# Second mixing stage: an earlier third weight load, weights split behind the product two rows ahead, and the decay chain and the heads five rows later

## The chip, the cores and the metric

The kernel runs on one NeuronCore of a Trainium2 chip. The metric is device time in microseconds (us) of one execution of the whole program; lower is better. TensorE (PE) multiplies, VectorE (DVE) and ScalarE (ACT) prepare operands and take results away, GpSimd (POOL) and SyncE (SP) start most transfers. The engines run their own instruction streams in order and wait for each other by semaphores.

## What is computed

The reference is two transformer blocks on 512 tokens of width 1024 in float32. The change touches only one stage of the second block, the first projections of its mixing and the gated delta rule behind them:

```python
h = modulate(x, g_mix[l], sh2, sc2)
proj = h @ w_in[l]
q_lat, kv_lat, k_pe, gq, gk, gv, ga, gb, gz, gates = jnp.split(proj, split_at, axis=-1)
...
qkv = jax.nn.silu(causal_depthwise_conv(qkv, w_conv))
q = l2norm(to_chunks(q, DK)) * (DK ** -0.5)
k = l2norm(to_chunks(k, DK))
beta = jax.nn.sigmoid(b.astype(f32))
g = -jnp.exp(a_log.astype(f32)) * jax.nn.softplus(a.astype(f32) + dt_bias.astype(f32))
decay = jnp.cumsum(g, axis=-1)
...
A = jnp.where(strict, jnp.einsum('bhnid,bhnjd->bhnij', k_beta, k) * L, 0.0)
T = lax.linalg.triangular_solve(A + eye, ...)
w = jnp.einsum('bhnij,bhnjd->bhnid', T, k_beta * jnp.exp(decay)[..., None])
u = jnp.einsum('bhnij,bhnje->bhnie', T, v * beta[..., None])
```

## The kernel before

**Rows.** The projection is done in 57 *rows*, numbered 0 to 56: each takes 128 columns of `w_in` against all of `h` and leaves one 128x512 result in PSUM bank 0 or 1 in turn. float32 is kept by splitting each operand into a rounded part and a rest: for row n, ScalarE rounds the weights (`w_hi`, line 222, tile `Wh`), VectorE makes the rest (`w_lo`, line 234, tile `Wl`), and TensorE runs 24 matmuls (`pe_three`, lines 242 to 244). There are two split slots, so `w_hi` of row n+2 can start only when the product of row n is done, and four raw slots, filled by SP's `w_load`. Row 0 and the small tile `t_ab` (40 columns: the heads' a and b) are multiplied together in `pe_two` (lines 427 to 430) while `h` is still being made piece by piece, eight pieces k.

Rows 0 to 5, 11 to 16, 25 to 30 and 39 to 44 are the key, query and value of two heads each. For these VectorE runs a four-tap convolution (`conv_dve`, lines 2523 and 2526), ScalarE a SiLU and, for key and query, a square (lines 2493, 2499); TensorE sums the squares over the partitions (line 2463), ScalarE takes the root (2484), VectorE the reciprocal and a diagonal (2547, 2549), TensorE spreads it (2451), and VectorE scales (2540). The other rows are latents, output gates and branch gates, which ScalarE takes away (lines 2777, 2506, 2514).

**Decay chain.** From the `t_ab` product come beta (sigmoid on ScalarE, line 2375) and the decays: abs, exp, ln, exp on ScalarE (2378 to 2383), then five operations on VectorE (2400 to 2408, mark `lx`), then 12 small transposes on TensorE (`decay_pe`), and the copies of `decay_act` and `decay_dve`. The heads need all of it.

**Heads.** Each of eight heads is a generator in 14 parts on TensorE, ScalarE and VectorE. In the *opening* TensorE spreads the decays of the head (lines 2602, 2603) and turns the values (171); VectorE subtracts and masks (2712 to 2717); ScalarE exponentiates and scales (2660 to 2669). The *second part* is the key-by-key and key-by-query products (2612, 2614, 171). In the *third part* VectorE makes the start of the triangular inverse (2724 to 2732) and TensorE turns it (line 2288, first 16 matmuls). Ten parts of doubling steps (2632, 2288, 2641) and a last part (2647, 2650) follow.

**Order.** `row_steps` writes the order out: step n holds the front of row n (its product on TensorE, norms), then one part of each of at most two live heads, then the back of row n (convolution or taking away). At most one head is started in a step, when the row of its values is past; head h+2 starts when head h has ended. The heads start in steps 3, 6, 17, 20, 31, 34, 45 and 48. Behind the rows six products for the keys of the other branch (line 251) are interleaved with the last head parts.

**Queues.** SP issues `t_ab` and rows 0 and 1, waits for the end of the stage ahead, then for all of `h`, and then issues a 512 KB constant (`sel8`), the 2 MB save of X (`x_out`), row 2 and the rest. `delta_act` starts with a wait for `x_out` on ScalarE, ahead of the rows' own loop; in the kernel before, row 2's split stands ahead of it in `mix2_act`.

Of the kernel before, what the change touches and what calls it, by code (L numbers as in the profile page):

```python
# [96 lines left out]
def build(nc, a, out, upto="end"):  # L97
# [285 lines left out]
    class Modulated:  # L383
# [33 lines left out]

        def pe_two(self, e, outs, ts, ms, keys):

            w = [[x.rearrange("p (k m) -> p k m", k=8) for x in w_parts(i)] for i in ts]  # L420
            steps = [(t, k) for k in range(6) for t in (0, 1)] + [(t, k) for t in (0, 1) for k in (6, 7)]
            for i in ts:
                V.wait_ge(e, ("w", i))
            for t, k in steps:
                o, (hi, lo) = outs[t][0:ms[t], :], w[t]
                A.wait_ge(e, (self.tag, "hi", k))
                e.matmul(o, hi[:, k, :], self.hi[:, k, :], start=k == 0, stop=False)
                e.matmul(o, lo[:, k, :], self.hi[:, k, :], start=False, stop=False)
                V.wait_ge(e, (self.tag, "lo", k))
                ins = e.matmul(o, hi[:, k, :], self.lo[:, k, :], start=False, stop=k == 7)  # L430
                if k == 7:
                    PE.then_inc(ins, ("w", ts[t]), keys[t])
# [1778 lines left out]
    NCX = 2  # L2211
# [108 lines left out]
    def mix2_sp(e):  # L2320
        for i in [t_ab] + t_row[0:2]:
            w_load(e, i)
        behind(e, "ffn1")
        con2_in.then_inc(e.dma_start(con1[:, 768:1344], a["consts"][:, 2048:2624]), "con2")
        A.wait_ge(e, ("m2", "hi", 7))
        V.wait_ge(e, ("m2", "lo", 7))
        sel_in.then_inc(e.dma_start(sel8, a["consts"][:, 3072:4096]), "sel")
        x_out.then_inc(e.dma_start(XD, X_t), "x")
        for i in t_row[2:] + t_uk:
            w_load(e, i)  # L2330

    def mix2_pe(e):
        m2n.root_pe(e)
        n4.pe_two(e, [ps(2), ps(0)], [t_ab, t_row[0]], (40, 128), ["ab", ("row", 0)])

# [34 lines left out]
    def mix2_act(e):  # L2370
        R = CX[0][0]
        n4.act(e)
        w_hi(e, t_row[1])
        PE.wait_ge(e, "ab")
        A.then_inc(e.activation(bb[0:8, :], ps(2)[32:40, :], ACT.Sigmoid), "bb")
        w_hi(e, t_row[2])
        V.wait_ge(e, "ab1")
        A.then_inc(e.activation(R[0:8, :], ab[0:8, :], ACT.Abs), "r1")
        A.wait_ge(e, "r1")
        A.then_inc(e.activation(R[0:8, :], R[0:8, :], ACT.Exp, scale=-1.0), "r2")  # L2380
        A.wait_ge(e, "r2")
        A.then_inc(e.activation(R[0:8, :], R[0:8, :], ACT.Ln, bias=1.0), "r3")
        A.then_inc(e.activation(ea[0:8, 0:1], vec("a_log")[0:8, :], ACT.Exp), "ea")

    def mix2_dve(e):
        R, SQ, LX = CX[0][0], CX[1][0], CXT[1][:, 512:1024]
        V.then_inc(e.scalar_tensor_tensor(out=wc4, in0=mod2[:, 32:40], scalar=1.0, in1=vec("g_mix_2"), op0=ADD, op1=MUL),
                   "wc4")
        V.wait_ge(e, "wc4")
        n4.dve(e, t_row[0])  # L2390
        w_lo(e, t_row[1])
        PE.wait_ge(e, "ab")
        V.then_inc(e.tensor_copy(ab[0:8, :], ps(2)[0:8, :]), "ab0")
        V.wait_ge(e, "ab0")
        V.then_inc(e.tensor_scalar(ab[0:8, :], ab[0:8, :], vec("dt_bias")[0:8, :], None, ADD), "ab1")
        conv_dve(e, 0)
        w_lo(e, t_row[2])
        A.wait_ge(e, "ea")
# [17 lines left out]
    def row_steps(rows, make_head):  # L2416
# [3 lines left out]
        while rows or todo or live:  # L2420
            if rows:
                n += 1
                if next(rows, "end") == "end":
                    rows, n = None, 99
            if todo and at_row["qkv", todo[0], 2] < n and len(live) < NCX:
                live.append(make_head(todo.pop(0)))
            live = [g for g in live if next(g, "end") != "end"]
            if rows:
                next(rows)

    NROW = len(ROWS)
    LAT = {"k": ("kl", 2), "q": ("ql", 6)}
# [6 lines left out]
    def rows_pe(e):  # L2439
        for n in range(NROW + 2):  # L2440
            if n < NROW:
                if n >= 2:
                    (V if ROWS[n - 2][0] == "qkv" else A).wait_ge(e, ("row_out", n - 2))
                if n:
                    pe_three(e, ps(n % 2), t_row[n], 8, 128, H4, 0, 8, ("row", n))
            if n == 2:
                decay_pe(e)
# [24 lines left out]
    def rows_act(e):  # L2472
        for n in range(NROW + 2):
            if 1 < n < NROW - 1:
                w_hi(e, t_row[n + 1])
            if n == 2:
                decay_act(e)
# [7 lines left out]
            if n in LSUM:  # L2485
                lat_root_act(e, LSUM[n])
            yield
            if n < NROW:
                kind, h, c = ROWS[n]
# [28 lines left out]
    def conv_dve(e, n):  # L2518
        _, h, c = ROWS[n]
        cv, w_ = part(h, c), wcv[:, c * 8 + h, :]  # L2520
        x_out.wait_ge(e, "x")
        PE.wait_ge(e, ("row", n))
# [7 lines left out]
    def rows_dve(e):  # L2530
        for n in range(NROW + 2):
            if 1 < n < NROW - 1:
                w_lo(e, t_row[n + 1])
            if n == 2:
                decay_dve(e)
# [19 lines left out]
            yield  # L2555
            if 0 < n < NROW and ROWS[n][0] == "qkv":
                conv_dve(e, n)
            elif n < NROW and ROWS[n][0] in ("kl", "ql"):
                lat_add_dve(e, ROWS[n][0][0], ROWS[n][1])
            yield  # L2560

# [1030 lines left out]
```

## Time and profile before

| | |
|---|---|
| time, median of 3 runs | 3248.88 us (3248.83 to 3248.94) |
| time of the profiled execution | 3245.86 us |
| its span in the profile | 3243.7 us |
| TensorE busy | 3139.2 us (97%) |
| VectorE busy | 2039.1 us (63%) |
| ScalarE busy | 1337.9 us (41%) |

The span is that of the instructions in the trace; 2.2 us of the profiled execution lie around it. Positions are in us from the start of the span. The stage that the change touches runs from about 2000 to 2509.

### The profile page before, as it was taken

The page shows a single profiled execution, that of the slowest core. Times are in us where ns is not written, and L with a number is a line of the kernel's source. Part 1 is how long each engine was busy: PE and PEld are TensorE (multiplying, and loading weights), DVE is VectorE, ACT ScalarE, POOL GpSimd, SP SyncE. Part 2 cuts the span into 40 slices and gives each one's busy share as a digit, 9 for nine tenths or more (in the row PEclk, how much of TensorE's full clock was granted, in tenths as well). Part 3 has the DMA queues.
Part 4 walks back from the last instruction along what each step waited for, and adds up shares of the span by engine and source line. Part 5 has one row for each costly group of instructions (what it writes and reads, how often), then busy time and mean ns, then how long its engine had stood idle before and what let it go on. Part 6 is the DMA issues. An engine that isn't in the chain of part 4 may idle for free.

```text
span 3243.7 us, 43188 instructions
## 1 busy us (share of the span) xinstructions
PE 3139.2 (97%) x17353; PEld 2614.5 (81%) x17353; DVE 2039.1 (63%) x3563; ACT 1337.9 (41%) x2348; POOL 580.1 (18%) x510
## 2 busy tenths in 40 slices
PE   8999999999999999999999999899999999999998
PEld 6865899898888888888878887688887566778887
DVE  6856878776888888888665553655452455443333
ACT  4352249884444444444432222554553224232322
POOL 1001359872222222222000000000000000000000
PEclk9999999999999999999899999899999999999999
DMA  7316245569999999999445552222222231322222
GB/s 279 115 55 231 86 146 184 200 223 354 336 335 330 328 334 328 331 330 339 141 154 183 192 174 95 71 71 93 92 76 79 78 112 56 104 84 94 97 95 80
DMA packets 190070, 574.41 MB, mean 177 GB/s; under 512 B 16304, under 2 KB 81968, under 8 KB 171568
## 3 DMA queue, kind: packets, MB, share of 16 engines
q1 hardware_dynamic: 152000, 367.83, 33.1%
q0 software_dynamic: 37872, 203.84, 17.6%
q8 instruction: 137, 2.24, 0.3%
q14 instruction: 61, 0.50, 0.0%
HBM read 523.76 MB, written 47.84 MB: 176 GB/s over the span
## 4 chain that ended last, share of the span: by engine, by line
PE 83%; DVE 6%; ACT 5%; DMA 4%; issue 1%; POOL 1%; SPq 0%; DVEq 0%; ACTq 0%; POOLq 0%
PE ps L242 12%; PE ps L243 12%; PE ps L244 12%; PE ps L1820 5%; PE ps L1821 5%; PE ps L1819 5%; PE ps L1574 4%; PE ps L1576 4%; PE ps L1575 4%; PE ps L251 2%; DMA hidden_dram<-peerg_HS 2%; DMA adaw_AW<-w_ada 1%; ACT Wh L222 1%; PE ps L774 1%; PE ps L775 1%
## 5 line engine op out<-in xcount | busy, mean ns | idle before, releaser
L234 DVE TENSOR_TENSOR Wl<-W,Wh 128x1024 fp32r<-128x1024 f32 (+1 forms) x354 | 429.2, 1213 | 662.6 <-ACT Wh L222 662.4
L222 ACT ACTIVATE Wh<-W 128x1024 fp32r<-128x1024 f32 x380 | 396.5, 1044 | 548.9 <-PE ps L244 507.3
L1574 PE MATMUL ps<-peer_Hh,Wh 128*128 128x384 f32 x1024 | 347.1, 339 | 2.2 <-DVE Wl L234 1.4
L1576 PE MATMUL ps<-peer_Hh,Wl 128*128 128x384 f32 x1024 | 343.5, 335 | 0.0
L1575 PE MATMUL ps<-peer_Hl,Wh 128*128 128x384 f32 x1024 | 343.1, 335 | 0.0
L1788 POOL DMA_INDIRECT peerv_UV<-peer_uv,peer_EX x128 | 210.5, 1644 | 638.0 <-DVE peer_Y L1860 584.2
L1821 PE MATMUL ps<-peerv_VH,peer_HTl 128*128 128x512 f32 x768 | 300.5, 391 | 0.0
L1819 PE MATMUL ps<-peerv_VH,peer_HTh 128*128 128x512 f32 x768 | 299.0, 389 | 1.3 <-DVE peer_HTl L1887 1.3
L1820 PE MATMUL ps<-peerv_VL,peer_HTh 128*128 128x512 f32 x768 | 300.3, 391 | 0.0
L242 PE MATMUL ps<-f_Hh,Wh 128*128 128x512 f32 x656 | 257.3, 392 | 5.7 <-DVE Wl L234 5.7
L243 PE MATMUL ps<-f_Hl,Wh 128*128 128x512 f32 x656 | 256.3, 391 | 0.0
L244 PE MATMUL ps<-f_Hh,Wl 128*128 128x512 f32 x656 | 256.3, 391 | 0.0
L1566 POOL TENSOR_SCALAR peerg_OH<-consts_sb,peert_IT,peert_GT 128x128 f32<-128x128 f32 x192 | 216.0, 1138 | 28.7 <-PE ps L1701 16.4
L242 PE MATMUL ps<-mix2h_Hh,Wh 128*128 128x512 f32 x512 | 208.0, 406 | 11.2 <-DVE Wl L234 5.0
L243 PE MATMUL ps<-mix2h_Hl,Wh 128*128 128x512 f32 x512 | 201.6, 394 | 0.0
L244 PE MATMUL ps<-mix2h_Hh,Wl 128*128 128x512 f32 x512 | 201.1, 393 | 0.0
L1574 PEld LDWEIGHTS ps<-peer_Hh,Wh 128*128 128x128 f32 x1024 | 192.7, 188 | 7.8 <-issue 2.7
L1575 PEld LDWEIGHTS ps<-peer_Hl,Wh 128*128 128x128 f32 x1024 | 192.7, 188 | 2.8
L1576 PEld LDWEIGHTS ps<-peer_Hh,Wl 128*128 128x128 f32 x1024 | 192.4, 188 | 0.0
L1753 DVE TENSOR_TENSOR peerv_VL<-peerv_VR,peerv_VH 128x1024 fp32r<-128x1024 f32 x128 | 156.7, 1224 | 48.3 <-ACT peerv_VH L1749 47.6
L1819 PEld LDWEIGHTS ps<-peerv_VH,peer_HTh 128*128 128x128 f32 x768 | 144.2, 188 | 32.8 <-DVE peer_HTl L1887 2.2
L1821 PEld LDWEIGHTS ps<-peerv_VH,peer_HTl 128*128 128x128 f32 x768 | 144.1, 188 | 30.3
(588 smaller groups left out, 6311.1 us busy)
## 6 DMA issues: line engine op xcount, KB each, us to landing
W<-peer_u SPq DMA_DIRECT2D x128, 512.0 KB, 6.9
peerv_VR<-peer_v SPq DMA_DIRECT2D x128, 512.0 KB, 5.3
f_AW<-w_ada POOLq DMA_DIRECT2D x56, 512.0 KB, 4.5
gates_dram<-peerg_GB SPq DMA_DIRECT2D x12, 2048.0 KB, 7.3
peerv_GR<-gates_dram SPq DMA_DIRECT2D x32, 768.0 KB, 7.9
W<-w_gate SPq DMA_DIRECT2D x44, 512.0 KB, 3.5
W<-w_up SPq DMA_DIRECT2D x44, 512.0 KB, 3.5
W<-w_down SPq DMA_DIRECT2D x32, 512.0 KB, 3.5
```

The lines of the kernel that those rows point to most:

```text
L222: A.then_inc(e.activation(w_parts(i)[0], w_raw(i), ACT.Copy), ("w_hi", i))
L234: (G if i in lo_on_pool else V).then_inc(e.tensor_tensor(lo, w_raw(i), hi.bitcast(F32), SUB), ("w", i))
L242: e.matmul(o[0:m, :], hi[:, j, :], rhs[0][:, k, :], start=k == 0, stop=False)
L243: e.matmul(o[0:m, :], hi[:, j, :], rhs[1][:, k, :], start=False, stop=False)
L244: ins = e.matmul(o[0:m, :], lo[:, j, :], rhs[0][:, k, :], start=False, stop=k == nk - 1)
L1566: ins = e.tensor_scalar(oh(q)[0][:, s, :], iota, IT[:, c:c + 1], GT[:, c:c + 1], EQ, MUL)
L1574: e.matmul(o, hi[:, k, :], H2[0][:, k, 0:TD], start=k == 0, stop=False)
L1575: e.matmul(o, hi[:, k, :], H2[1][:, k, 0:TD], start=False, stop=False)
L1576: ins = e.matmul(o, lo[:, k, :], H2[0][:, k, 0:TD], start=False, stop=k == 7)
L1819: e.matmul(o, HTh[:, s, sl], VH[:, s, d], start=n == 0, stop=False)
L1820: e.matmul(o, HTh[:, s, sl], VL[:, s, d], start=False, stop=False)
L1821: ins = e.matmul(o, HTl[:, s, sl], VH[:, s, d], start=False, stop=n == 127)
```

## The change

- SP issues the load of row 2 with those of `t_ab`, rows 0 and 1, ahead of the end of the stage before.
- `pe_two` runs `t_ab` three pieces ahead of row 0 (argument `lag`).
- The split of row n+2 (`w_hi`, `w_lo`) is issued at the back of step n: on ScalarE ahead of the SiLU or the taking away of row n, on VectorE behind the convolution of row n. Before, it was issued at the front of step n+1.
- The decay chain leaves the entrance of the stage: `rate_act` and `rate_dve` come in step 5 (`RATE`), `decays_dve` and `decay_pe` in step 6, `decay_act` and `decay_dve` in step 7.
- No head starts before step 7, so the heads start in steps 7, 8, 21, 22, 35, 36, 49 and 50.
- Only value rows wait for `x_out` on VectorE; row 0's convolution moves from `mix2_dve` into the rows' loop.

```diff
-        def pe_two(self, e, outs, ts, ms, keys):
+        def pe_two(self, e, outs, ts, ms, keys, lag=0):
             w = [[x.rearrange("p (k m) -> p k m", k=8) for x in w_parts(i)] for i in ts]
             steps = [(t, k) for k in range(6) for t in (0, 1)] + [(t, k) for t in (0, 1) for k in (6, 7)]
+            if lag:
+                steps = [(t, k - t * lag) for k in range(8 + lag) for t in (0, 1) if 0 <= k - t * lag < 8]
...
     def mix2_sp(e):
-        for i in [t_ab] + t_row[0:2]:
+        for i in [t_ab] + t_row[0:3]:
             w_load(e, i)
...
-        for i in t_row[2:] + t_uk:
+        for i in t_row[3:] + t_uk:
             w_load(e, i)
...
     def mix2_act(e):
-        R = CX[0][0]
         n4.act(e)
         w_hi(e, t_row[1])
+
+    def rate_act(e):
+        R = CX[0][0]
         PE.wait_ge(e, "ab")
         A.then_inc(e.activation(bb[0:8, :], ps(2)[32:40, :], ACT.Sigmoid), "bb")
-        w_hi(e, t_row[2])
         V.wait_ge(e, "ab1")
...
-        conv_dve(e, 0)
-        w_lo(e, t_row[2])
+
+    def decays_dve(e):
+        R, SQ, LX = CX[0][0], CX[1][0], CXT[1][:, 512:1024]
         A.wait_ge(e, "ea")
...
-            if todo and at_row["qkv", todo[0], 2] < n and len(live) < NCX:
+            if todo and max(at_row["qkv", todo[0], 2], RATE + 1) < n and len(live) < NCX:
                 live.append(make_head(todo.pop(0)))
...
-    NROW = len(ROWS)
+    NROW, RATE = len(ROWS), 5
...
-            if n == 2:
+            if n == RATE + 1:
                 decay_pe(e)
...
     def rows_act(e):
         for n in range(NROW + 2):
-            if 1 < n < NROW - 1:
-                w_hi(e, t_row[n + 1])
-            if n == 2:
+            if n == RATE:
+                rate_act(e)
+            if n == RATE + 2:
                 decay_act(e)
...
             yield
+            if n + 2 < NROW:
+                w_hi(e, t_row[n + 2])
             if n < NROW:
...
     def conv_dve(e, n):
...
-        x_out.wait_ge(e, "x")
+        if c == 2:
+            x_out.wait_ge(e, "x")
...
     def rows_dve(e):
         for n in range(NROW + 2):
-            if 1 < n < NROW - 1:
-                w_lo(e, t_row[n + 1])
-            if n == 2:
+            if n == RATE:
+                rate_dve(e)
+            if n == RATE + 1:
+                decays_dve(e)
+            if n == RATE + 2:
                 decay_dve(e)
...
-            if 0 < n < NROW and ROWS[n][0] == "qkv":
+            if n < NROW and ROWS[n][0] == "qkv":
                 conv_dve(e, n)
             elif n < NROW and ROWS[n][0] in ("kl", "ql"):
                 lat_add_dve(e, ROWS[n][0][0], ROWS[n][1])
+            if n + 2 < NROW:
+                w_lo(e, t_row[n + 2])
```

The order of the instructions on the engines shows where the moved work comes to stand. In the changed file the lines of this stage lie 2 to 13 numbers further down, so that 2523 is 2531 there, 2484 is 2489, 2493 is 2500, 2660 is 2672 and 2724 is 2736.

ScalarE at the entrance of the stage, before: from the split of row 1 to the squares of row 0's SiLU.

```order
L222 ACTIVATE Wh<-W 128x1024 [waits pe_done,w_in2]
L2375 ACT_TABLE_LOAD
L2375 ACTIVATE gdnh_b<-ps 8x512
L222 ACTIVATE Wh<-W 128x1024 [waits pe_done,w_in3]
L2378 ACTIVATE gdnh_c<-gdnh_a 8x512 [waits dve_done]
L2380 ACT_TABLE_LOAD
L2380 ACTIVATE gdnh_c<-gdnh_c 8x512 [waits act_done]
L2382 ACT_TABLE_LOAD
L2382 ACTIVATE gdnh_c<-gdnh_c 8x512 [waits act_done]
L2383 ACT_TABLE_LOAD
L2383 ACTIVATE gdnh_ea<-vecs_sb 8x1
```

ScalarE in steps 4 and 5 of the changed kernel: from the square of row 4 to the split of row 7.

```order
L2506 ACTIVATE gdnc_AN<-gdnq_QD 128x512 [waits act_done]
L2379 ACT_TABLE_LOAD
L2379 ACTIVATE gdnh_b<-ps 8x512
L2381 ACTIVATE gdnh_c<-gdnh_a 8x512 [waits dve_done]
L2383 ACT_TABLE_LOAD
L2383 ACTIVATE gdnh_c<-gdnh_c 8x512 [waits act_done]
L2385 ACT_TABLE_LOAD
L2385 ACTIVATE gdnh_c<-gdnh_c 8x512 [waits act_done]
L2386 ACT_TABLE_LOAD
L2386 ACTIVATE gdnh_ea<-vecs_sb 8x1
L2489 ACT_TABLE_LOAD
L2489 ACTIVATE small<-ps,small 128x4 [waits pe_done]
```

The chain has moved in one piece, and the root of row 4's norm (L2489) now stands behind it.

VectorE in steps 5 and 6 of the changed kernel: from the reciprocal that waits for that root, over the convolution of row 5 and the split of row 7, to the end of the decay chain (the row L2413 carries the mark `lx`).

```order
L2557 RECIPROCAL small<-small 128x4 [waits act_done]
L2559 TENSOR_TENSOR DG<-consts_sb,small 128x512 [waits dve_done]
L2531 TENSOR_SCALAR X<-ps,vecs_sb 128x512
L2534 SCALAR_TENSOR_TENSOR X<-ps,vecs_sb,X 128x511 [waits dve_done]
L2534 SCALAR_TENSOR_TENSOR X<-ps,vecs_sb,X 128x510 [waits dve_done]
L2534 SCALAR_TENSOR_TENSOR X<-ps,vecs_sb,X 128x509 [waits dve_done]
L234 TENSOR_TENSOR Wl<-W,Wh 128x1024 [waits act_done]
L2405 SCALAR_TENSOR_TENSOR gdnh_a<-gdnh_a,gdnh_c 8x512
L2407 TENSOR_SCALAR gdnh_a<-gdnh_a,gdnh_ea 8x512 [waits dve_done]
L2409 SCALAR_TENSOR_TENSOR gdnh_c<-consts_sb,gdnh_a 8x512 [waits dve_done]
L2411 COPY gdnh_a<-gdnh_c 8x512 [waits dve_done]
L2413 TENSOR_TENSOR gdnh_c<-gdnh_c 8x512
```

Before, these last five stood behind the split of row 2 and ahead of the convolution of row 1.

VectorE at the third part of head 2, before (step 19): the two splits ahead of it are those of rows 19 and 20; the last opening ahead of it is the head's own, two steps earlier.

```order
L2784 TENSOR_TENSOR mix_ZG<-mix_ZG 128x512 [waits act_done]
L234 TENSOR_TENSOR Wl<-W,Wh 128x1024 [waits act_done]
L2757 TENSOR_TENSOR gdnh_sel<-gdnh_c,ps 64x4x64 [waits pe_done]
L2757 TENSOR_TENSOR gdnh_sel<-gdnh_c,ps 64x4x64
L2784 TENSOR_TENSOR mix_ZG<-mix_ZG 128x512 [waits dve_done,act_done]
L234 TENSOR_TENSOR Wl<-W,Wh 128x1024 [waits act_done]
L2724 SCALAR_TENSOR_TENSOR gdnh_c<-ps,gdn_tc,gdnh_c 128x64 [waits pe_done]
L2724 SCALAR_TENSOR_TENSOR gdnh_c<-ps,gdn_tc,gdnh_c 128x64 x3
```

The same place in the changed kernel (steps 22 and 23): the rows L2724 to L2729 are here the opening of head 3, L234 is the split of row 24, and the four L2736 begin the third part of head 2.

```order
L2724 TENSOR_TENSOR gdnh_c<-gdn_tc,ps 64x256 [waits pe_done]
L2724 TENSOR_TENSOR gdnh_c<-gdn_tc,ps 64x256
L2727 TENSOR_TENSOR gdnc_AN<-gdnh_c,consts_sb 128x4x64 [waits dve_done]
L2729 TENSOR_TENSOR gdnh_c<-gdnh_c,consts_sb 128x256 [waits dve_done]
L234 TENSOR_TENSOR Wl<-W,Wh 128x1024 [waits act_done]
L2736 SCALAR_TENSOR_TENSOR gdnh_c<-ps,gdn_tc,gdnh_c 128x64 x4
L2740 TENSOR_TENSOR gdnh_c<-gdnh_c,consts_sb 128x256 [waits dve_done]
```

The opening of the pair's other head now lies between a head's opening and its third part; on ScalarE the rounding of row 24 (`Wh`), for which this L234 waits, stands behind the whole of that opening.

## Rows read from the trace of the kernel before

**Rows 1.** TensorE's waits, 2000 to 2530: us in total, times, longest.

```profile
PE ps L242 <- DVE Wl L234: 5.0, 4, 2.3
PE ps L242 <- DVE gdn_tc L2363: 4.7, 1, 4.7
PE ps L2288 <- DVE gdnc_AN L2732: 3.4, 1, 3.4
...
PE ps L2463 <- ACT gdnc_AN L2499: 2.5, 1, 2.5
...
PE ps L2612 <- DVE gdnq_QD L2540: 0.9, 1, 0.9
```

**Rows 2.** Busy us in stretches: length, PE, PEld, DVE, ACT, POOL, then PEclk, DMA share.

```profile
2031.00:2034.50 3.50, 3.33 (x8) 2.68 (x9) 0.03 (x1) 3.45 (x4) 0.00 (x0) 0.51 0.44 157
2045.00:2048.00 3.00, 2.98 (x7) 2.42 (x8) 1.06 (x3) 2.46 (x9) 0.00 (x0) 0.50 0.56 175
2065.40:2073.00 7.60, 6.61 (x51) 6.04 (x52) 5.51 (x8) 4.68 (x6) 0.00 (x0) 0.57 0.19 69
2082.10:2086.00 3.90, 3.81 (x23) 3.19 (x24) 3.87 (x9) 2.43 (x5) 0.00 (x0) 0.56 0.02 4
2120.00:2520.00 400.00, 397.75 (x3603) 320.12 (x3602) 200.99 (x356) 192.32 (x324) 16.71 (x30) 1.00 0.26 86
```

**Rows 3.** TensorE's timeline, rows 1 to 4: start, us, idle before.

```profile
2023.09 0.50 PE L242 MATMUL ps<-mix2h_Hh,Wh 128*128 128x512 f32 x1 [1.09 <-DVE Wl L234]
...
2052.02 1.02 PE L2451 MATMUL ps<-DG,consts_sb 128*128 128x512 f32 x2
...
2053.76 0.49 PE L2602 MATMUL ps<-gdnh_ah,gdnh_selr 8*128 8x512 f32 x1
...
2056.40 0.47 PE L242 MATMUL ps<-mix2h_Hh,Wh 128*128 128x512 f32 x1 [1.33 <-DVE Wl L234]
...
2061.97 1.02 PE L2451 MATMUL ps<-DG,consts_sb 128*128 128x512 f32 x2
```

**Rows 4.** Timeline of ScalarE and VectorE around the decay chain, 2023 to 2050.

```profile
2023.09 0.59 ACT L2375 ACTIVATE gdnh_b<-ps 8x512 f32<-8x512 f32 x1
...
2026.79 0.75 DVE L2523 TENSOR_SCALAR gdnc_KD<-ps,vecs_sb 128x512 f32<-128x512 f32 x1 [2.65 <-DMA x_dram<-X]
...
2028.81 0.61 ACT L2378 ACTIVATE gdnh_c<-gdnh_a 8x512 f32<-8x512 f32 x1
...
2029.81 1.22 DVE L234 TENSOR_TENSOR Wl<-W,Wh 128x1024 fp32r<-128x1024 f32 x1
...
2034.85 0.68 DVE L2400 SCALAR_TENSOR_TENSOR gdnh_a<-gdnh_a,gdnh_c 8x512 f32<-8x512 f32 x1 [3.82 <-ACT gdnh_ea L2383]
...
2036.13 0.63 ACT L2493 ACTIVATE gdnc_KD<-gdnc_KD 128x512 f32<-128x512 f32 x1
...
2037.66 0.67 DVE L2408 TENSOR_TENSOR gdnh_c<-gdnh_c 8x512 f32<-8x512 f32 x1
...
2049.68 0.69 DVE L2549 TENSOR_TENSOR DG<-consts_sb,small 128x512 f32<-128x512 f32 x1
```

**Rows 5.** Timeline of all engines around head 2's opening and third part, 2181 to 2195.

```profile
2181.26 0.49 PE L2602 MATMUL ps<-gdnh_ah,gdnh_selr 8*128 8x512 f32 x1
...
2182.97 1.28 ACT L2660 ACT_TABLE_LOAD   x1 [1.21 <-DVE gdnh_c L2712]
...
2185.63 1.12 ACT L2669 ACTIVATE X<-ps,gdn_tc 128x128 f32<-128x128 f32 x4
...
2187.59 1.09 ACT L222 ACTIVATE Wh<-W 128x1024 fp32r<-128x1024 f32 x1
...
2187.99 0.68 PE L2641 MATMUL ps<-gdnh_c 64*64 64x64 f32 x16
...
2192.72 0.86 DVE L2724 SCALAR_TENSOR_TENSOR gdnh_c<-ps,gdn_tc,gdnh_c 128x64 f32<-128x64 f32 x4
...
2194.41 0.42 DVE L2732 TENSOR_TENSOR gdnc_AN<-ps,gdnc_AN 128x256 f32<-128x256 f32 x1
```

More of the change, by code:

```diff
@@ L2333, in mix2_pe @@
         m2n.root_pe(e)
-        n4.pe_two(e, [ps(2), ps(0)], [t_ab, t_row[0]], (40, 128), ["ab", ("row", 0)])
+        n4.pe_two(e, [ps(2), ps(0)], [t_ab, t_row[0]], (40, 128), ["ab", ("row", 0)], 3)
     def decay_pe(e):
@@ L2385, in mix2_dve @@
     def mix2_dve(e):
-        R, SQ, LX = CX[0][0], CX[1][0], CXT[1][:, 512:1024]
         V.then_inc(e.scalar_tensor_tensor(out=wc4, in0=mod2[:, 32:40], scalar=1.0, in1=vec("g_mix_2"), op0=ADD, op1=MUL),
@@ L2391, in mix2_dve, with rate_dve @@
         w_lo(e, t_row[1])
+    def rate_dve(e):
         PE.wait_ge(e, "ab")
```

## The prediction

> **What bounds the kernel now.** I read the page first: TensorE is busy for almost the whole span, so a change can only give or take where TensorE stands idle or runs at its lower clock. Then the table of stretches and TensorE's waits for the stage that is changed. From 2120 to 2520 TensorE is busy 397.75 us of 400 at a granted clock of 1.00, the level of 2.4 GHz [rows 2]: the steady rows with heads running beside them lose nothing, although VectorE and ScalarE work only half of that time. All that can be won lies ahead of it, between 2022 and 2108. There the waits are 5.0 us in four waits for `Wl` of a row, 4.7 for the entrance with the decay chain, 2.5 and 0.9 behind squares and scaling, and 3.4 for head 0's third part [rows 1]: 16.5 us in all. Behind four of them the granted clock stands at 0.50 to 0.57 (0.5 is the level of 1.2 GHz) [rows 2]. Work at half clock takes twice as long, so busy time times (1 - clock) is lost: 3.33 x 0.49 + 2.98 x 0.50 + 6.61 x 0.43 + 3.81 x 0.44 = 7.6 us. **The kernel before loses 24.1 us here.** A perfect change gets these back, no more.
>
> **What a row costs.** At full clock a row's product and the start of the next work are 5.57 us apart (2056.40 to 2061.97), a spread and a sum of squares together 1.74 (2052.02 to 2053.76) [rows 3]. A wait of 1.1 (ahead of 2023.09) or 1.33 (ahead of 2056.40) is followed by matmuls of 0.47 to 0.50, near full speed [rows 3]; one of 2.3 and longer is followed by half clock [rows 1, 2]. Such a stretch costs 1.5 to 1.7 where a row follows, 2.8 where small head matmuls and a second wait follow.
>
> **The change, part by part.**
>
> *Row 1.* `t_ab` ends six matmuls earlier in `pe_two`, so the split slot for row 1 is free earlier, and the wait of 1.1 goes. The number of matmuls stays. That feeding one tile alone for three pieces makes TensorE wait or keeps its clock low longer is not shown by any row; I take 0, with 1.5 as the upper end (one more half-clock stretch) and 0 as the lower, since the work is the same.
>
> *Row 2.* Its weights are now there early, but ScalarE meets `delta_act`'s wait for `x_out` before it may split them. VectorE was released by the save of X at 2026.79 [rows 4]. Now a rounding (1.09 [rows 5]) and a rest (1.22 [rows 4]) follow, so row 2 starts at 2029.1. Row 1 starts at 2022.0 (2023.09 less its wait) and ends at 2027.5. A wait of 1.6 remains, and a half-clock stretch that lies between the cases seen (1.33: none; 2.3: full): I take half of 1.6. Term 2.4; bounds 0.6 (the save lands 1 us earlier, as one load fewer is queued with it) and 3.2.
>
> *Rows 3 to 6.* From the end E of a row's product, VectorE and ScalarE need: spread and sum 1.74, root 0.3 (estimate, a 128x4 operation), reciprocal and diagonal 0.9 (the diagonal 0.69), convolution 3.02 (2026.79 to 2029.81), rest of the weights 1.22 [rows 3, 4]. That is E + 7.2. TensorE wants those weights at E + 1.74 + 5.57 + 1.74 = E + 9.0. The SiLU and square (twice 0.63 [rows 4]) end at E + 7.3, as the next row's product does, a spread ahead of the sum that needs them. So the split behind the product does what it says: 0. The cover is 1.8 us; were it gone, each of four rows would cost what is missing.
>
> *The decay chain.* It leaves the entrance, but in steps 5 and 6 it stands in three engines' order. ScalarE starts it after the square of row 4, at the end of row 5's product (call it F, by the line above). A table load 1.28 [rows 5], sigmoid 0.59, then 7.32 from the abs at 2028.81 to the SiLU at 2036.13, which holds three exponentials or logarithms and four more loads [rows 4], then the root of row 4's norm, 0.3: F + 9.5. Queued behind this root on VectorE are reciprocal and diagonal 0.9, the convolution of row 5 3.02, the split of row 7 1.22, and only then the chain's own five operations, 2034.85 to 2038.33, 3.48 [rows 4]: `lx` at F + 18.1. TensorE has spread and sum 1.74 and row 6, 5.57, and then stands at `decay_pe`, ahead of row 7, at F + 7.3. **A wait of 10.8**, with one half-clock stretch of 1.5: 12.3. Bounds 9 and 14: F rests on two ends that fall together within a few tenths, and on an estimated root; 2 us either way is more than the row steps ahead can add or take.
>
> The trace shows each load at 1.28 us and no gap behind it that the 7.32 does not hold. The Trainium skill, "ScalarE: Activation LUTs", section What ACT_TABLE_LOAD costs, puts a change of table at about 2.66 us, the load of 1283 ns and a drain of about 1380 ns. By that, five loads would make this wait 6.9 us longer and the time about 3272.5; the rows decide, and the sum goes without it.
>
> *Heads one step apart.* Head 0's opening is in step 7, head 1's in step 8, and so for every pair. Take a pair (4 and 5). From the start of the second head's opening TensorE has this opening and a row, 6.73 us (2181.26 to 2187.99 [rows 5]), and then wants the first head's third part. ScalarE has the whole opening, 5.49 (2181.26 to 2186.75, with a table load inside), and behind it the rounding of the next weights, 1.09; VectorE then their rest, 1.22 [rows 4], and only behind that the third part, 2.11 (2192.72 to 2194.83) [rows 5]: 9.9. **A wait of 3.2 on line 2288**, and half clock on the small head matmuls behind it: between 1.5 and 2.8, I take 2.0. For the three later pairs 3 x 5.2 = 15.6, which before is hidden, since the heads start three steps apart and no opening comes between. Lower end 3 x 3.2 (no loss of clock), upper 3 x 6.0 (the 2.8 seen).
>
> *The first pair.* In step 9 the root of the latent norm stands ahead of head 0's third part, as a key's norm did in step 5 of the kernel before; that wait was 3.4 [rows 1], so 3.4 and 2.0. In step 10 two scalings of 128x512 (0.69 each, taken from the diagonal of that size [rows 4]) wait for a spread and stand ahead of head 1's third part: 1.4 + 2.1 less a head part of some 0.5 on TensorE, 3.0 and 1.6. Together 10.0, bounds 5 and 13.
>
> *The end.* The last heads end in step 63 instead of 61, the six key products fill steps 59 to 64. Two steps stand without a row beside two heads; TensorE's waits have no row for lines 2632 or 2641 anywhere in the stage, and each step now has two heads' matmuls to cover one head's copies. I take 0.2, with 2 as the upper end (half of a third part for each step).
>
> **Sum.** After: 0 + 2.4 + 0 + 12.3 + 15.6 + 10.0 + 0.2 = 40.5. Before: 24.1. **16.4 us more.** On the profiled execution's 3245.86 (span 3243.7 and what lies around it) this makes 3262.3; that run lies 3.0 below the median of the runs, 3248.88, so the median becomes **3265.3**, 0.5% slower.
>
> **The rivals.**
>
> *Third parts covered (faster).* If VectorE reaches the third part before TensorE asks for it, because it is let past the split, all five waits on line 2288 go: 15.6 + 10.0 less. 3239.7. It decides at an opening of ScalarE 3.2 us shorter than 5.49. For it: in the kernel before, heads 2 to 7 show no such wait. Against it: there the opening lay two steps ahead, and the order of the engines fixes the split between. 1 in 10.
>
> *One of the two big terms missing (no change).* Without the wait at `decay_pe`, 12.3 less, 3253.0; without the three later pairs, 15.6 less, 3249.7. The first would need ScalarE to be 10.8 us ahead of VectorE's convolution, the second what the rival above needs, in the plain rows alone, where ScalarE only takes results away and may get through the opening sooner. 1.2 in 10 together.
>
> *Both heads of a pair wait (slower still).* If the first head's late third part makes the second head's late too, a wait of about 3.2 with 2.0 comes once more in each of three pairs, 15.6 more: 3280.9; for one or two pairs 3270 to 3276. Against it: between them TensorE has a second part at half clock and a row, some 9 us, for some 7 of VectorE. 1.2 in 10.
>
> **The numbers.** The forecast has 6.6 in 10, within 3257 to 3273. A measurement of this kernel can tell about 0.2%, 6.5 us, from no change. Faster by that is the first rival, 0.10; within it most of the second, 0.12; the rest, 0.78, is slower. The range 3252 to 3275 takes in the bounds of the terms, each near its end, and the upper part of the second rival and lower part of the third.
>
> **What the changed profile shows.** Right: no wait on line 242 ahead of rows 1 and 3 to 6; one on `decay_pe`'s first transpose (line 171) of 9 to 12 us; five on the line that was 2288, of 3 to 4 us, ahead of head parts in steps 9, 10, 23, 37 and 51; granted clock near 0.5 behind each. Wrong: the stretch of the later heads still at 1.00 and full, a wait at `decay_pe` under 5, or waits moved onto `Wl`, which would say that the splits and not the heads' order carry the loss.

## The result, and the profile after

The changed kernel takes 3263.08 us (median of 5 runs, 3261.48 to 3273.21) against 3248.94 us of the kernel before (5 runs): ratio 1.0043, 95% interval 1.003 to 1.0057. It is slower by 0.43%. The profiled execution took 3262.14 us, with a span of 3259.1.

TensorE's waits in the stage of the changed kernel, us in total, times, longest; they answer to [rows 1]:

```profile
PE ps L2290 <- DVE gdnc_AN L2744: 15.4, 5, 4.2
PE ps L171 <- DVE gdnh_c L2413: 10.8, 1, 10.8
PE ps L242 <- DVE Wl L234: 3.4, 2, 3.1
```

The waits for squares and scaling (2.5 and 0.9 before) are gone, and of the four for weights two are left. In their place stand one long wait at the decay transposes (line 171) and five at the third parts (line 2290, which was 2288). TensorE's timeline has the places (start, us, idle before):

```profile
2008.85 0.62 PE L429 MATMUL ps<-mix2h_Hh,Wh 128*40 128x512 f32 x1 [1.81 <-ACT mix2h_Hh L397]
...
2031.11 0.59 PE L242 MATMUL ps<-mix2h_Hh,Wh 128*128 128x512 f32 x1 [3.12 <-DVE Wl L234]
2046.72 0.47 PE L242 MATMUL ps<-mix2h_Hh,Wh 128*128 128x512 f32 x1 [0.27 <-DVE Wl L234]
2077.75 0.27 PE L171 MATMUL ps<-consts_sb,gdnh_a 8*128 8x8 f32 x1 [10.83 <-DVE gdnh_c L2413]
2107.54 1.12 PE L2290 MATMUL ps<-consts_sb,gdnh_c 64*64 64x64 f32 x16 [4.15 <-DVE gdnc_AN L2744]
2122.41 0.68 PE L2290 MATMUL ps<-consts_sb,gdnh_c 64*64 64x64 f32 x16 [3.00 <-DVE gdnc_AN L2744]
2230.57 0.68 PE L2290 MATMUL ps<-consts_sb,gdnh_c 64*64 64x64 f32 x16 [3.21 <-DVE gdnc_AN L2744]
2345.43 1.12 PE L2290 MATMUL ps<-consts_sb,gdnh_c 64*64 64x64 f32 x16 [2.53 <-DVE gdnc_AN L2744]
2462.21 0.68 PE L2290 MATMUL ps<-consts_sb,gdnh_c 64*64 64x64 f32 x16 [2.53 <-DVE gdnc_AN L2744]
...
2525.56 1.37 PE L3022 MATMUL ps<-gdnr_S,mix_YG 128*64 128x128 f32 x16 [2.07 <-DVE gdnr_S L3061]
```

The first row shown is the first matmul of `t_ab`, the last one the first of the state loop behind the stage. Between them lie 516.7 us; in the kernel before 503.3 (2008.01 to 2511.28). **The stage is 13.4 us longer.** The other 2 us of the two spans' difference lie ahead of it and behind it, in code that is the same. In the profiles of this study the stage begins anywhere between 2005.5 and 2019.1, so whole times carry differences that no edit here made; below, kernels are compared by the length of this stage first.

Stretches behind the waits (length, PE, PEld, DVE, ACT, POOL, PEclk, DMA share), to be read beside [rows 2]:

```profile
2031.00:2035.00 4.00, 3.89 (x10) 3.13 (x11) 3.89 (x5) 2.85 (x5) 0.00 (x0) 0.57 0.42 142
...
2077.50:2082.00 4.50, 4.25 (x17) 3.00 (x18) 0.96 (x3) 0.00 (x0) 0.00 (x0) 0.50 0.00 0
2107.50:2111.50 4.00, 3.96 (x53) 3.75 (x54) 2.63 (x8) 2.79 (x7) 0.00 (x0) 0.50 0.03 6
2122.00:2126.00 4.00, 3.59 (x24) 2.95 (x25) 2.80 (x8) 2.43 (x6) 0.00 (x0) 0.68 0.00 0
2230.00:2234.00 4.00, 3.43 (x58) 3.11 (x59) 3.11 (x10) 2.26 (x6) 0.00 (x0) 1.00 0.41 166
2345.00:2349.00 4.00, 3.58 (x58) 3.49 (x60) 3.11 (x9) 2.41 (x6) 0.00 (x0) 0.57 0.38 153
2462.00:2466.00 4.00, 3.79 (x69) 3.40 (x70) 3.11 (x9) 2.58 (x6) 0.00 (x0) 1.00 0.36 143
```

Busy time times (1 - clock) gives 1.7, 2.1, 2.0, 1.1, 0, 1.5 and 0. With the waits of 29.6 us this is 38.0 us lost, against 24.1 before: 13.9 more, and the stage's lengths say 13.4.

Where the 10.8 us come from is read on ScalarE and VectorE in steps 5 and 6:

```profile
2059.84 1.28 ACT L2379 ACT_TABLE_LOAD   x1
...
2067.66 1.28 ACT L2489 ACT_TABLE_LOAD   x1
2068.95 0.26 ACT L2489 ACTIVATE small<-ps,small 128x4 f32<-128x4 f32 x1
...
2069.25 0.18 DVE L2557 RECIPROCAL small<-small 128x4 f32<-128x4 f32 x1 [7.93 <-ACT small L2489]
...
2073.08 1.22 DVE L234 TENSOR_TENSOR Wl<-W,Wh 128x1024 fp32r<-128x1024 f32 x1
2074.21 0.67 DVE L2405 SCALAR_TENSOR_TENSOR gdnh_a<-gdnh_a,gdnh_c 8x512 f32<-8x512 f32 x1
...
2077.02 0.67 DVE L2413 TENSOR_TENSOR gdnh_c<-gdnh_c 8x512 f32<-8x512 f32 x1
```

ScalarE is in the chain from 2059.84 to 2067.6, then comes the root of row 4's norm. VectorE stands 7.93 us for that root, then does reciprocal, diagonal, convolution and split, and only then the chain's own five operations, though the last input of these was ready at 2067.6.

The pair of heads 2 and 3, all engines, at the third part of head 2:

```profile
2220.59 0.49 PE L2614 MATMUL ps<-gdnh_ah,gdnh_selr 8*128 8x512 f32 x1
...
2225.96 1.07 ACT L222 ACTIVATE Wh<-W 128x1024 fp32r<-128x1024 f32 x1
...
2227.06 1.22 DVE L234 TENSOR_TENSOR Wl<-W,Wh 128x1024 fp32r<-128x1024 f32 x1 [3.92 <-ACT Wh L222]
2228.32 0.86 DVE L2736 SCALAR_TENSOR_TENSOR gdnh_c<-ps,gdn_tc,gdnh_c 128x64 f32<-128x64 f32 x4
```

Head 3's opening starts at 2220.59; the rounding on ScalarE stands behind all of it, VectorE waits 3.92 us for that rounding, and head 2's third part stands behind the split. Its start at 2228.32 is 2.25 us ahead of TensorE's 2230.57: in the order predicted, with the wait of 3.2 predicted.

### The profile page after: what moved, and what is told of

The parts are those of the page before. It is cut to its first block, busy times and chain, and to the rows that moved or that the text cites. A ratio compares the mean times of both kernels' runs of the same rounds, so it can differ in the third digit from the quotient of the medians.

```text
span 3259.1 us, 43189 instructions
## 1 busy us (share of the span) xinstructions
PE 3140.0 (96%) x17353; PEld 2614.4 (80%) x17353; DVE 2036.4 (62%) x3563; ACT 1338.2 (41%) x2348; POOL 580.2 (18%) x510
## 4 chain that ended last, share of the span: by engine, by line
PE 83%; DVE 7%; ACT 5%; DMA 4%; issue 1%; POOL 1%; SPq 0%; DVEq 0%; ACTq 0%; POOLq 0%
PE ps L242 12%; PE ps L243 11%; PE ps L244 11%; PE ps L1822 5%; PE ps L1823 5%; PE ps L1821 5%; PE ps L1576 4%; PE ps L1578 4%; PE ps L1577 4%; PE ps L251 2%; DMA hidden_dram<-peerg_HS 2%; DMA adaw_AW<-w_ada 1%; ACT Wh L222 1%; PE ps L776 1%; PE ps L777 1%
## 5 line engine op out<-in xcount | busy, mean ns | idle before, releaser
L234 DVE TENSOR_TENSOR Wl<-W,Wh 128x1024 fp32r<-128x1024 f32 (+1 forms) x354 | 428.5, 1211 | 602.1 <-ACT Wh L222 601.2
```

The source lines that it names most:

```text
L234: (G if i in lo_on_pool else V).then_inc(e.tensor_tensor(lo, w_raw(i), hi.bitcast(F32), SUB), ("w", i))
```

## The experiments

Stage lengths, from the first matmul of `t_ab` to the first of the state loop, in the one profiled execution of each kernel, and times. Where several runs were timed, the ratio to the kernel before has its interval; the others are single runs. The two columns behind the stage are read from the same profiles: TensorE's idle time in the stage, and busy time times (1 - clock), summed over stretches of 3 us. Both hold what every kernel has at the two ends of the stage: 2 us of wait ahead of the state loop, some 3 us of slow clock at the entrance.

| kernel | stage us | idle us | lost by clock us | time us | ratio |
|---|---|---|---|---|---|
| before | 503.3 | 18.8 | 10.1 | 3248.9 | |
| changed | 516.7 | 32.0 | 12.4 | 3263.1 | 1.0043 (1.003 to 1.0057) |
| heads_three | 516.0 | 27.9 | 14.1 | 3262.3 | 1.0046 (1.0033 to 1.006) |
| heads_two | 520.2 | 32.1 | 15.4 | 3266.9 | 1.0054 (1.004 to 1.0068) |
| three_step6 | 498.8 | 16.8 | 8.9 | 3234.1 | |
| before_heads_late | 527.0 | 36.3 | 17.9 | 3268.0 | |
| before_splits | 499.4 | 15.0 | 10.2 | 3240.1 | |
| chain_spread | 507.5 | 21.9 | 12.9 | 3247.9 | 1.0 (0.9991 to 1.0009) |
| decay_late | 511.9 | 25.6 | 13.3 | 3259.6 | |
| chain_first | 513.9 | 27.1 | 14.6 | 3268.9 | |
| no_save_wait | 514.1 | 28.8 | 13.5 | 3254.0 | 1.0023 (1.0014 to 1.0033) |
| no_lag | 513.9 | 30.6 | 10.9 | 3261.1 | |
| pieces_three_step6 | 484.0 | 6.0 | 4.5 | 3226.6 | 0.9931 (0.9918 to 0.9943) |
| select_early | 482.4 | 4.2 | 4.6 | 3224.3 | 0.9923 (0.9902 to 0.9945) |

What is left of a stage without these two columns is 472 to 474 us in every kernel, so they account for the differences in length to within 3 us. Whole times of single runs do not: chain_first has the shorter stage and the longer time, because its stage begins 10.3 us later than the changed kernel's.

**Heads: how far apart, and beside which rows.** The start of a pair's second head is held back by two or three steps:

```diff
-        todo, live, n = list(range(8)), [], -1
+        todo, live, n, last = list(range(8)), [], -1, -9
...
-            if todo and max(at_row["qkv", todo[0], 2], RATE + 1) < n and len(live) < NCX:
+            if todo and max(at_row["qkv", todo[0], 2], RATE + 1) < n and len(live) < NCX and n >= last + 3:
                 live.append(make_head(todo.pop(0)))
+                last = n
```

> The changed kernel with the second head of a pair started no earlier than three steps behind the first (steps 7, 10, 21, 24, ...), all else the same. Theory: the waits on line 2290 in the later pairs come from the other head's opening one step behind, which holds ScalarE ahead of the next split. Then the three later waits (3.2, 2.5 and 2.5 us) and about 1.5 of half clock behind them go, and the one in step 10 (3.0 and 1.1) too; the one in step 9 (4.2) stays, because the root of the latent norm stands ahead of it whatever the other head does; the last head ends two steps later, which costs 1 to 2 us. About 3251 us. Rival: the waits come from the heads lying five steps later, beside other kinds of rows; then all five stay and the time is 3263 to 3265.

> The changed kernel with the second head of a pair two steps behind the first (steps 7, 9, 21, 23, ...), all else the same. Theory: two steps are enough, since the second opening then comes behind the first head's third part on VectorE and ScalarE; the same waits go as with three steps, and the last head ends one step later only: about 3250 us. Rival: the openings of 5.5 us fill ScalarE wherever they lie, and the second head's opening in the same step as the third part makes another split late: waits of 2 to 3 us on line 242 or 2290 stay once in each pair, 3256 to 3260.

Both expectations failed. With three steps 10.5 us of waits stay on line 2290, with two 15.4, and the loss by clock is 1.7 and 3.0 us above the changed kernel's. But the waits stand at other heads and behind other work. VectorE with three steps between (step 26), then TensorE:

```profile
2244.63 0.18 DVE L2558 RECIPROCAL small<-small 128x4 f32<-128x4 f32 x1 [3.03 <-ACT small L2490]
2244.84 0.69 DVE L2560 TENSOR_TENSOR DG<-consts_sb,small 128x512 f32<-128x512 f32 x1
2245.45 0.85 DVE L2737 SCALAR_TENSOR_TENSOR gdnh_c<-ps,gdn_tc,gdnh_c 128x64 f32<-128x64 f32 x4
...
2247.70 0.68 PE L2290 MATMUL ps<-consts_sb,gdnh_c 64*64 64x64 f32 x16 [2.33 <-DVE gdnc_AN L2745]
```

and with two steps between (step 25):

```profile
2250.66 0.42 DVE L2766 TENSOR_TENSOR gdnh_c<-gdnh_c,ps 128x256 f32<-128x256 f32 x1 [4.35 <-PE ps L2654]
...
2251.34 0.85 DVE L2737 SCALAR_TENSOR_TENSOR gdnh_c<-ps,gdn_tc,gdnh_c 128x64 f32<-128x64 f32 x4
...
2253.59 1.12 PE L2290 MATMUL ps<-consts_sb,gdnh_c 64*64 64x64 f32 x16 [2.97 <-DVE gdnc_AN L2745]
```

With three steps, the third part of head 3 falls into step 26, where the reciprocal of row 25's norm stands ahead of it and waits 3.03 us for a root; the same happens in steps 12 and 40, and at the latent's norm in step 9 (3.53). The last pair's third parts, beside which no row has a norm, wait for nothing. With two steps, the other head is at a doubling step, and VectorE waits for that product (L2654), which TensorE runs just before it asks for the third part. So the spacing is not the cause by itself. That gave a new theory: what counts is whether anything that waits for another engine stands ahead of the third part on VectorE. The kernel for it has three steps between, as above, and chain and heads one step earlier.

```diff
-    NROW, RATE = len(ROWS), 5
+    NROW, RATE = len(ROWS), 4
```

> The changed kernel with the second head three steps behind the first and everything of the decay chain and the heads one step earlier (RATE 4: chain from step 4, heads in steps 6, 9, 20, 23, ...). Read in the stage, from the first matmul of row 0's line to the first of the state loop behind it: 516.7 us in the changed kernel, 503.3 in the kernel before, 516.0 with three steps between but heads from step 7. Theory: a third part on VectorE makes TensorE wait in a step in which something stands ahead of it on VectorE that waits for another engine: a split whose rounding stands behind the other head's opening (one step between), the other head's subtraction behind a doubling product (two between), or the reciprocal of a row's or latent's norm (heads from step 7 with three between: steps 9, 12, 26, 40). From step 6 the third parts fall in steps 8, 11, 22, 25, 36, 39, 50 and 53, where no norm is; so all waits on line 2290 go (10.5 us and 2 to 3 of half clock), the 10.8 at the decay transposes stays: stage 502 to 504. Rival: the third parts wait for their own long VectorE work wherever they stand; then 2 to 3 us stay three or four times, stage 510 to 515.

Its waits in the stage, the two largest:

```profile
PE ps L171 <- DVE gdnh_c L2413: 11.2, 1, 11.2
...
PE ps L242 <- DVE Wl L234: 3.0, 2, 2.7
```

There is no wait on line 2290 at all, and the stage takes 498.8 us, 17.2 less than with the heads one step later. That is 3 us below the range expected, since 5.2 us of loss by clock went with the waits instead of 2 to 3. The rival falls, and that late work ahead of the third part is the cause is shown. The theory's wording is too strong, though. Splits that wait for ScalarE also stand right ahead of third parts for which TensorE does not wait; here that of head 3,

```profile
2225.53 1.23 DVE L234 TENSOR_TENSOR Wl<-W,Wh 128x1024 fp32r<-128x1024 f32 x1 [0.84 <-ACT Wh L222]
```

and the same head in the kernel before:

```profile
2215.18 1.23 DVE L234 TENSOR_TENSOR Wl<-W,Wh 128x1024 fp32r<-128x1024 f32 x1 [1.78 <-ACT Wh L222]
```

So it is not a wait as such that counts, but how late VectorE is released from it. The run also says that the decay stall of 11.2 us can be in a kernel that is faster than the one before.

The heads' late start alone, put into the kernel before:

```diff
-            if todo and at_row["qkv", todo[0], 2] < n and len(live) < NCX:
+            if todo and max(at_row["qkv", todo[0], 2], 6) < n and len(live) < NCX:
```

> The kernel before with one part of the change alone: no head starts before step 7, so heads start in steps 7, 8, 21, 22, ...; the decay chain stays in the entrance, splits and loads as before. Theory: the heads' order alone costs what the changed kernel shows on line 2290, 15.4 us of waits in five places and about 5 of half clock, less the wait of 3.4 and the 1.7 behind it that the kernel before has at head 0: stage 516 to 520 against 503.3. Rival: those waits need the splits in their new place (behind a step's own row); with splits at the front of the next step the third part comes first, and the stage is 500 to 505.

```profile
PE ps L2288 <- DVE gdnc_AN L2732: 21.3, 5, 5.3
PE ps L242 <- DVE Wl L234: 8.0, 6, 2.6
```

527.0 us, 23.7 more than the kernel before and 10.3 more than the changed one: more than the theory gave, and the rival falls. The later pairs wait 4.4 to 5.3 us here instead of 2.5 to 3.2, and the waits for weights are 8.0 against 5.0.

**The splits alone.** In the kernel before, `w_hi` and `w_lo` of rows 3 on move to the back of the step two rows ahead, as in the change; nothing else.

```diff
-            if 1 < n < NROW - 1:
-                w_hi(e, t_row[n + 1])
...
             yield
+            if 0 < n and n + 2 < NROW:
+                w_hi(e, t_row[n + 2])
...
```

> The kernel before with one part of the change alone: the splits of rows 3 on at the back of the step two rows ahead; chain, heads, loads and row 2's split as before. Theory: this part is the gain in the change. The kernel before with the heads late needs 527.0 us for the stage, the changed one, which has the splits moved too, 516.7; so here the waits of 5.0 us on line 242, with the half clock behind them, fall by half or more: stage 498 to 501 against 503.3. Rival: the gain of the new place shows only where heads lie one step apart; with heads three apart there is none, stage 503 to 504.

```profile
PE ps L2463 <- ACT gdnc_AN L2499: 3.7, 1, 3.7
PE ps L2288 <- DVE gdnc_AN L2732: 3.4, 1, 3.4
PE ps L242 <- DVE Wl L234: 3.4, 2, 2.3
PE ps L242 <- DVE gdn_tc L2363: 2.3, 1, 2.3
```

499.4 us, as the theory gave, though by other shares: the waits for weights fall by 1.6 us, not by half, the one for the entrance by 2.4 and the one for scaling goes (0.9); the one for a square grows by 1.2. This part of the change is a gain of 3.9 us, all of it in waits (idle time 3.8 less, loss by clock the same), and the heads' order hid it.

**The decay chain.** Three kernels, each from the changed one. The chain in three pieces on ScalarE, behind the split and ahead of the SiLU, and VectorE's part at the front of step 5 (`rate_act` now does the sigmoid for n = 2, the abs and both exponentials for n = 3, the logarithm for n = 4):

```diff
-            if n == RATE:
-                rate_act(e)
...
             if n + 2 < NROW:
                 w_hi(e, t_row[n + 2])
+            rate_act(e, n)
...
-            if n == RATE:
+            if n == RATE - 2:
                 rate_dve(e)
-            if n == RATE + 1:
+            if n == RATE:
                 decays_dve(e)
```

> The changed kernel with the decay chain in three pieces on ScalarE, at the backs of steps 2, 3 and 4 between the split and the SiLU, where ScalarE stands idle for a convolution, and VectorE's five operations at the front of step 5; TensorE's decay transposes stay where they are, behind row 6. Theory: the 10.8 us wait comes from the chain standing in one lump in the order, with the next root, convolution and split behind it; in pieces it is hidden, the wait falls to 1 or less with its 2.1 of half clock: about 3250.5 us. Rival: ScalarE has no room in the first rows, the pieces with their extra table loads make the splits of rows 5 to 7 late, and 4 to 7 us come back as waits on line 242: 3255 to 3258.

The wait of 10.8 is gone. New waits are 0.7 for a square and 0.6 for a constant's rounding, and no row waits for weights that did not before. The stage is 9.2 us shorter, where 12.9 was expected: 10.0 of waits went, but the loss by clock did not fall with them. The 2.1 behind the decay wait went, and in its stead the clock was low behind all three waits of the later pairs instead of one; these are as long as in the changed kernel (the rows are in the last section).

The transposes one step later, and in the same way their copies and the earliest start of a head:

```diff
-            if n == RATE + 1:
+            if n == RATE + 2:
                 decay_pe(e)
```

> The changed kernel with the decay transposes on TensorE, their copies and the heads one step later (transposes behind row 7, heads from step 8), the chain on ScalarE and VectorE where it is. Theory: the lump of the chain holds the split of row 7 too; that split ends at F+14.6, where TensorE can take row 7 at F+9.0, so most of the wait of 10.8 on line 171 turns into one of about 5.6 on line 242 ahead of row 7, and the transposes then wait for nothing. Rival: only the transposes are late; then no wait on line 242, and 3 to 4 us are left on line 171.

```profile
PE ps L2290 <- DVE gdnc_AN L2744: 13.7, 4, 5.4
PE ps L242 <- DVE Wl L234: 5.0, 3, 2.6
...
PE ps L2456 <- DVE DG L2559: 3.3, 1, 3.3
```

Line 171 waits for nothing, but 3.3 us stand now at the spread of row 4's norm, whose diagonal is behind the chain, and 2.17 of the 5.0 ahead of row 7: 5.4 us, as large as the theory said, on two lines instead of one. The lump delays all that is queued behind it; the transposes were only the last to ask.

VectorE's five operations ahead of step 5's reciprocal, convolution and split:

```diff
             if n == RATE:
                 rate_dve(e)
-            if n == RATE + 1:
                 decays_dve(e)
```

> The changed kernel with VectorE's five operations of the decay chain ahead of step 5's reciprocal, diagonal, convolution and split instead of behind them; ScalarE as it is. Theory: the 10.8 us are the chain's nine us on ScalarE and the row work queued ahead of its end on VectorE; the last of the five operations then ends about 6.5 us earlier, the wait on line 171 falls to 4 to 5, and 3 to 4 come back as a wait on line 242 ahead of row 7, whose split is now behind: stage 513 to 515 against 516.7. Rival: ScalarE's part alone sets the end; then line 171 keeps 9 or more.

Line 171 waits 4.26 us, and 2.16 us are new ahead of row 7: stage 513.9, as the theory gave. Of the 10.8 us, 6.6 were the queue on VectorE.

**The entrance.** ScalarE's wait for the save of X ahead of its rows is taken out; VectorE still waits for the save ahead of each value row, and ScalarE's work on those rows behind VectorE.

```diff
     def delta_act(e):
-        x_out.wait_ge(e, "x")
         row_steps(chain(rows_act(e), keys_act(e)), lambda h: head_act(e, h))
```

> The changed kernel without ScalarE's wait for the save of X ahead of its row loop; the rows of values still wait for it on VectorE, and ScalarE's work on them behind VectorE. Theory: the waits of 3.1 and 0.3 us ahead of row 2, with 1.2 of slower clock, come from that wait standing ahead of row 2's rounding; all go: about 3258.5 us. Rival: the weights of row 2 come late, or VectorE's rest does for another reason; then the wait stays, 3262 to 3264.

The 3.1 ahead of row 2 are gone and row 2 runs at clock 1.00; the 0.3, which lie ahead of row 4, stay. The stage is 2.7 us shorter, less than the 4.6 expected. The idle time fell by 3.2, as it should; the loss by clock rose by 1.1. Behind the three later waits on line 2290, as long as in the changed kernel, the clock is 0.69, 0.64 and 0.58 here in stretches of 4 us, 3.9 us lost against 1.5, and behind the decay wait it stays low longer. This takes back more than the 1.7 that row 2 gained in clock.

The old order of the two products:

```diff
-        n4.pe_two(e, [ps(2), ps(0)], [t_ab, t_row[0]], (40, 128), ["ab", ("row", 0)], 3)
+        n4.pe_two(e, [ps(2), ps(0)], [t_ab, t_row[0]], (40, 128), ["ab", ("row", 0)])
```

> The changed kernel with the two products of the entrance in their old order (no lag of three pieces between them), all else the same. Theory: the wait of 1.1 us on line 242 ahead of row 1 that the kernel before has comes back and nothing else changes: stage 517 to 518 against 516.7. Rival: row 1's split was early enough through the other edits; then no wait ahead of row 1 and the same stage within 0.3.

```profile
2025.45 0.50 PE L242 MATMUL ps<-mix2h_Hh,Wh 128*128 128x512 f32 x1 [1.09 <-DVE Wl L234]
2031.70 0.47 PE L242 MATMUL ps<-mix2h_Hh,Wh 128*128 128x512 f32 x1 [0.50 <-DVE Wl L234]
```

The wait of 1.09 came back, but the stage is 2.8 us shorter, not longer: row 2 waits 0.50 instead of 3.12 and starts at full speed. With the lag row 1 starts 1.5 us earlier in the stage, but row 2 cannot, since the save holds its split, and the save lands 1.0 us later. So the time won ahead of row 1 is waited for ahead of row 2, with 1.0 us more, and the clock behind this one wait is 0.57. Neither theory had this.

**Together.** Chain in pieces, no wait for the save, three steps between heads, all one step earlier; and then the heads' selection constant rounded at the back of step 4 instead of behind the decay copies.

> The changed kernel with the chain in three pieces on ScalarE (backs of steps 1, 2 and 3, VectorE's part at the front of step 4), no wait for the save of X ahead of ScalarE's rows, heads from step 6 and three steps between the heads of a pair. Theory: the three causes are separate and add up; what is left of lost time in the stage is 3 to 5 us (the kernel before 24.1, the changed one 37.5), stage 482 to 485, time 3227 to 3231, faster than both kernels. Rival: the pieces in the first rows, beside two waits for norms each, make splits late again, 3 to 6 us more: 3232 to 3236.

> The kernel of the run pieces_three_step6 (stage 484.0 us, 3226.6) with the rounding of the selection constant for the heads (1.04 us on ScalarE) at the back of step 4 instead of behind the decay copies. Theory: its wait of 2.4 us ahead of head 0's opening is the largest left in the stage; of it about 1 goes, the length of that rounding, since the opening then waits for the split rest of the decays instead: stage 482.5 to 483.5, time 3225 to 3227. Rival: the added 1.04 us delays the squares of row 4 and a wait of the same size comes there; stage 484 to 485.

The first takes 484.0 us in the stage. The three parts tried alone (three_step6, chain_spread, no_save_wait) shorten the changed kernel's stage by 17.9, 9.2 and 2.7, 29.8 in all; together it is 32.7, so the causes add up to within 3 us. Its largest wait left is the 2.4 us for that constant; in the second only 0.6 are left there, and the stage takes 482.4. Both are faster than the kernel before; their intervals overlap, so that they differ is read from the stage alone.

## Why the prediction was right, and where it was not

The direction and the size were right: 16.4 us slower forecast, 13.4 in the stage and 14.1 by the medians. The sum is closer than its terms, and that is luck: row 2 came out 2.4 us higher than forecast and the later pairs 5.8 lower.

- *Row 1* (0): the wait went, and the clock at the entrance was no lower for it (2.7 us lost in the first 18 us of the stage, 3.0 before). It was no gain either, as no_lag shows.
- *Row 2* (2.4): a wait of 3.1 and 1.7 of clock, 4.8, above the bound of 3.2. That the save fixes row 2's start was right; its length was not. The save took 9.9 us, not the 8.9 taken from the kernel before, and no_lag, where it takes 8.9 again, shows that the lag did this, the part reckoned at 0 for row 1. And the clock behind the wait was 0.57, where half a slow stretch was taken.
- *Rows 3 to 6* (0): one wait of 0.27, ahead of row 4.
- *Decay chain* (12.3): 10.8 and 2.1. The queue was as worked out; chain_first and decay_late show it by moving one piece each.
- *First pair* (10.0): waits of 4.15 and 3.00, half clock 3.1, so 10.3. That the latent's norm causes the first is borne out: with no other opening near, heads_three still waits 3.53 there. Ahead of the second stand the two scalings, waiting for the spread, as forecast:

```profile
2118.83 1.40 DVE L2830 SCALAR_TENSOR_TENSOR mix_KL<-mix_KL,vecs_sb,ps 128x512 f32<-128x512 f32 x2 [5.70 <-PE ps L2808]
```

- *Later pairs* (15.6): 8.3 of waits and 1.5 of clock, 9.8. For heads 4 to 7 TensorE asks later, in part because it turns a head's values in 16 matmuls there (1.09 us in head 5 against 0.66 in head 3), so 2.5 instead of 3.2; and the clock fell behind one of three, not behind each. The last holds for this profile: in chain_spread and no_save_wait it fell behind each of the same three waits.
- *The reason given for the later pairs* was half right. An opening one step behind does cause these waits, but "the heads start three steps apart and no opening comes between" is not why the kernel before is free of them: at three steps they came back behind norms. In the kernel before, the splits right ahead of the third parts of heads 2 to 7 wait 1.78 us at most, and VectorE is there in time.
- *The end* (0.2): no wait.
- None of the three rivals happened: both big terms came, and the second heads of the later pairs do not wait.

The Trainium skill, "ScalarE: Activation LUTs", section What ACT_TABLE_LOAD costs, adds a drain of about 1380 ns to each change of table. The trace agrees with its load (1283 ns there, 1.28 us here) and shows no drain: the load at 2067.66 ends at 2068.94 and the root starts at 2068.95. By that page's figure, as an estimate, five drains would have made the forecast 6.9 us higher, 3272.2 by its own sum and not the 3272.5 written there; the wait came out at 10.83 us, near the 10.8 worked out from rows without a drain.

## What to carry to other kernels

On engines that work in order, the place of a short dependent step is judged by how late the operations ahead of it are released by other engines, not by its distance from the work that feeds it; list those for each step of the schedule before choosing starts. A chain of small operations with long latency belongs in pieces into gaps of its engine, since as a lump it delays everything queued behind it, whoever is seen to wait. A wait that is removed ahead of a row whose successor hangs on something else only moves, and two short waits can be cheaper than one long one (here 1.09 and 0.50 us at full clock against 3.12 with 0.57 behind it).

## What the runs showed of the hardware

The save of X (2 MB) took 8.8 to 8.9 us in the four profiles without the lag and 9.4 to 9.9 in the ten with it. The transfers of these two kernels, the changed one ahead:

```profile
x_dram<-X SPq DMA_DIRECT2D x1, 2048.0 KB, 9.9
```

```profile
x_dram<-X SPq DMA_DIRECT2D x1, 2048.0 KB, 8.9
```

The second is no_lag. With the lag row 1's split is done 1.6 us earlier in the stage, so its raw slot is free earlier and a row's load can start beside the save; that this is the cause fits but was not tried alone. And the granted clock did not follow the length of the wait: in the changed kernel it is 0.50 behind one of 4.15 us, 1.00 behind one of 3.21, 0.57 and 1.00 behind two of 2.53. Nor is it the same behind the same wait. The last three of these waits come back, equally long, in chain_spread, and the clock is low behind each:

```profile
2217.50:2221.50 4.00, 3.44 (x54) 3.19 (x55) 3.11 (x10) 2.27 (x6) 0.00 (x0) 0.75 0.39 158
2334.00:2338.00 4.00, 3.52 (x63) 3.48 (x64) 3.12 (x10) 2.36 (x6) 0.00 (x0) 0.69 0.39 158
2451.00:2455.00 4.00, 3.63 (x58) 3.55 (x60) 3.11 (x9) 2.47 (x6) 0.00 (x0) 0.58 0.38 154
```

These stretches lose 3.5 us, those of the changed kernel 1.5. So a stage's length can carry some 2 us that follow the clock and not the waits. Why is open.
